# A three-block transformer kernel: the Fourier branch folded by symmetry, and half of a later layer's modulation computed in another stage

## The chip, the cores and the metric

The kernel runs on one core of one Trainium2 chip. The metric is the device time in microseconds of one execution; times without a unit are microseconds. PE is TensorE, PEld its weight load, DVE VectorE, ACT ScalarE, POOL GpSimd, SP SyncE, whose queue issues most DMAs. PS is the PSUM, eight banks of 128 x 512 fp32. Steps are counted from 0; "step n" is the body of the attention's loop for n.

## The reference, cut to what matters

512 tokens of 1024 features pass through a first block (attention beside a Fourier branch, then a mixture of 32 experts) and a second one of two layers (an S5 state space mixer with a gated unit and an MLP; a Mamba-2 mixer and an MLP). The change touches two computations. The Fourier branch of the first block:

```
def fourier_mix(f, w_fourier):
    fg = f.reshape(b, n, N_FOURIER_GROUPS, FOURIER_GROUP_DIM)          # 512 tokens, 4 groups of 128
    fr = jnp.fft.fft2(fg, axes=(1, 3), norm='ortho').real
    return jnp.einsum('bngc,gcd->bngd', fr, w_fourier)
```

and the modulation of the second block's first layer:

```
mod = silu(c) @ ada_w[i] + ada_b[i]                                    # 1024 -> 6 x 1024
sh1, sc1, g1, sh2, sc2, g2 = split(mod, 6)
h = rmsnorm(x) * (1 + sc1) + sh1;  x = x + g1 * s5_mixer(h)            # ends in val * sigmoid(gate)
h = rmsnorm(x) * (1 + sc2) + sh2;  x = x + g2 * mlp(h)
```

## The kernel before

Activations lie features-first: 128 features on the partitions, 512 tokens along the row. All engines run programs written out by hand; each engine works through its own list in order, and semaphores tie the lists together. There is no planner: what stands earlier in an engine's list is done earlier.

**The attention** has four heads of four query tiles, sixteen steps n (`hd = n // 4`, `qc = n % 4`). In each step TensorE computes the scores of step n (`scores`, L931), turns the weights of step n-1 in two parts (`turn_weights`, L943), and between these does other work: in steps 0 to 3 the values' projections (`values`), in steps 4 to 7 the four groups of Fourier features (`to_mix`, both end in L840), in steps 8 to 13 the Fourier branch, in steps 14 and 15 parts of the output projection (`out_part`, L969). The values of a head are summed in steps 1 and 2 of the next head (`head_values`, L957); for heads 1 and 2 this waits for `head_done`, the scaling of the head before on DVE. DVE takes the maximum (`maxima`, L2234), ACT the two exponentials (`exps`, L1664), DVE the weights (`attention_weights`, L2242 to L2248); scores of step n wait for the exponentials of step n-1. At steps 8 and 12 DVE and ACT also finish a head's norm: `head_var` (DVE), `head_root` (ACT, with a load of the root's table), `head_scale` (DVE, a 512-column reciprocal L2260 and the product L2263).

**The Fourier branch**, per group: `mix_channels` multiplies the features by a 128 x 256 table of cosines and sines (four matmuls of 256 columns), ACT copies the result (`mixed_channels`), `mix_tokens` multiplies by the 512 x 512 cosine and sine tables over tokens (eight matmuls of 512 columns, L908 and L909), ACT copies (`mixed_tokens`), `mix_out` applies `w_fourier` (L916), ACT copies (`mixed_out`).

**Modulation** is a dot product on DVE: blocks of 128 output features, each a 128 x 1024 tile of transposed weights times the broadcast condition, summed along the row (`mod_block`, L2230). All 48 blocks of the layer are done in the attention, three a step, from two buffers; GpSimd issues their DMAs (L613) as `ada_used` frees a buffer. SyncE issues the expert weights only behind the last head's values and the last block.

**The gated unit** follows the S5 mixer: two halves i of the features, each as 4 value tiles (s = 0, banks 0 to 3) and 4 gate tiles (s = 1, banks 4 to 7), every product as three fp32r matmuls (L740 to L744). ACT takes the sigmoid of a gate tile (L1895), DVE the product with the value tile and the addition to x (L2677, L2680), which raises `glu_used`. TensorE writes bank k of the second half only when `glu_used` has reached k + 1. The norm ahead of the MLP needs all eight. The modulation of the second layer is done in the MLP, from `ada_buf1`.

## Time and profile before

| | |
|---|---|
| median of 3 runs (lowest, highest) | 2213.03 (2212.02, 2213.48) |
| the profiled execution's own time | 2213.58 |
| its span | 2211.9 |
| busy: PE, DVE, ACT, POOL | 2134.6, 1215.4, 702.6, 148.8 |
| DMA in the mean | 197 GB/s |
| attention, scores of step 0 to the turn of step 15's weights | 118.05 to 295.74 |
| gated unit on TensorE | 1004.11 to 1091.28 |

The profiler's page gives busy time by engine, granted TensorE clock, DMA load, the chain of work that ended last, and the costliest groups of instructions. Queries of the trace give the same for a stretch, and the instructions in order of time. Busy time of an engine off the chain costs nothing by itself. A matmul's busy time contains its way through the array; from the start of one to the start of the next is what it costs.

### The profile page before, as it was taken

The page shows a single profiled execution, that of the slowest core. Times are in us where ns is not written, and L with a number is a line of the kernel's source. Part 1 is how long each engine was busy: PE and PEld are TensorE (multiplying, and loading weights), DVE is VectorE, ACT ScalarE, POOL GpSimd, SP SyncE. Part 2 cuts the span into 40 slices and gives each one's busy share as a digit, 9 for nine tenths or more (in the row PEclk, how much of TensorE's full clock was granted, in tenths as well). Part 3 has the DMA queues.
Part 4 walks back from the last instruction along what each step waited for, and adds up shares of the span by engine and source line. Part 5 has one row for each costly group of instructions (what it writes and reads, how often), then busy time and mean ns, then how long its engine had stood idle before and what let it go on. Part 6 is the DMA issues. An engine that isn't in the chain of part 4 may idle for free.

```text
span 2211.9 us, 24806 instructions
## 1 busy us (share of the span) xinstructions
PE 2134.6 (97%) x9914; PEld 1428.7 (65%) x9914; DVE 1215.4 (55%) x1726; ACT 702.6 (32%) x1059; POOL 148.8 (7%) x157
## 2 busy tenths in 40 slices
PE   7999998997999989999999999999999999999997
PEld 3454444333333335678888888878777788888886
DVE  1776863344433336895474555566986646343434
ACT  4123422110000005323242231346884424232331
POOL 0011100002310004000000000000110000000000
PEclk9999999999999999999999999999999999999999
DMA  9756465999999993211345454423342222222221
GB/s 389 288 185 215 142 241 208 401 427 427 420 426 426 428 427 127 79 68 62 133 160 186 156 177 163 143 77 116 126 156 81 96 95 77 95 95 95 95 96 57
DMA packets 112808, 434.71 MB, mean 197 GB/s; under 512 B 7982, under 2 KB 13106, under 8 KB 98760
## 3 DMA queue, kind: packets, MB, share of 16 engines
q1 hardware_dynamic: 92872, 361.46, 42.6%
q0 software_dynamic: 19840, 71.93, 9.0%
q8 instruction: 66, 1.08, 0.2%
q14 instruction: 30, 0.25, 0.0%
HBM read 430.57 MB, written 6.36 MB: 198 GB/s over the span
## 4 chain that ended last, share of the span: by engine, by line
PE 60%; PEld 15%; DVE 7%; DMA 7%; issue 6%; ACT 2%; DVEq 2%; POOLq 0%; SPq 0%; PEldq 0%; POOL 0%; ACTq 0%
PE PS L1132 7%; PE PS L740 6%; PE PS L743 6%; PE PS L744 6%; PE PS L840 6%; PEld PS L740 5%; PEld PS L744 5%; PEld PS L743 4%; DMA work<-in_w_dn 4%; PE PS L1155 4%; PE PS L1399 3%; PE PS L1403 3%; PE PS L1402 3%; PE PS L1169 2%; PE PS L969 2%
## 5 line engine op out<-in xcount | busy, mean ns | idle before, releaser
L744 PE MATMUL PS<-work_f32r,work_f32r 128*128 128x512 f32 x1168 | 454.4, 389 | 0.0
L2155 DVE TENSOR_TENSOR ring_f32r<-ring,work_f32r 128x2048 fp32r<-128x2048 f32 x100 | 227.8, 2287 | 140.5 <-ACT work_f32r L1553 140.1
L740 PE MATMUL PS<-work_f32r,work_f32r 128*128 128x512 f32 x768 | 299.5, 390 | 2.1 <-DVE work_f32r L2902 1.1
L743 PE MATMUL PS<-work_f32r,ring_f32r 128*128 128x512 f32 x768 | 298.8, 389 | 0.0
L1553 ACT ACTIVATE work_f32r<-ring 128x2048 fp32r<-128x2048 f32 x100 | 190.2, 1910 | 304.0 <-DMA ring<-in_mlp_w 247.0
L744 PEld LDWEIGHTS PS<-work_f32r,work_f32r 128*128 128x128 f32 x1168 | 219.3, 188 | 45.6
L1132 PE MATMUL PS<-work 128*64 128x512 f32 x752 | 170.6, 597 | 2.2 <-ACT work L1761 2.2
L740 PEld LDWEIGHTS PS<-work_f32r,work_f32r 128*128 128x128 f32 x768 | 144.2, 188 | 33.3 <-DVE work_f32r L2902 1.5
L743 PEld LDWEIGHTS PS<-work_f32r,ring_f32r 128*128 128x128 f32 x768 | 144.2, 188 | 29.8 <-issue 0.2
L740 PE MATMUL PS<-h_f32r,work_f32r 128*128 128x512 f32 x400 | 155.9, 390 | 1.4 <-DVE work_f32r L2175 1.4
L743 PE MATMUL PS<-h_f32r,ring_f32r 128*128 128x512 f32 x400 | 155.6, 389 | 0.0
L2472 DVE SCALAR_TENSOR_TENSOR x<-PS,mod,x 128x512 f32<-128x512 f32 x128 | 90.1, 746 | 68.7 <-PE PS L1169 68.3
L1771 ACT ACTIVATE work<-PS 128x256 f32<-128x256 f32 x32 | 12.3, 383 | 360.3 <-PE PS L1132 360.3
L2717 DVE SCALAR_TENSOR_TENSOR x<-PS,mod,x 128x512 f32<-128x512 f32 x64 | 48.1, 751 | 137.2 <-PE PS L744 137.0
L1399 PE MATMUL PS<-h_f32r,work_f32r 128*128 128x512 f32 x288 | 120.7, 419 | 0.0
L1132 PEld LDWEIGHTS PS<-work 128*64 128x64 f32 x752 | 51.3, 137 | 101.9 <-issue 100.9
L1553 ACT ACTIVATE work<-PS 128x512 f32<-128x512 f32 (+2 forms) x94 | 50.8, 550 | 198.8 <-PE PS L840 85.9
L1403 PE MATMUL PS<-work_f32r,work_f32r 128*128 128x512 f32 x288 | 112.6, 391 | 0.0
L1402 PE MATMUL PS<-h_f32r,ring_f32r 128*128 128x512 f32 x288 | 112.4, 390 | 0.0
L2708 DVE TENSOR_SCALAR work<-PS 128x512 f32<-128x512 f32 x64 | 43.9, 691 | 116.0 <-PE PS L744 116.0
L1155 PE MATMUL PS<-work 128*64 128x512 f32 x384 | 94.7, 610 | 6.1 <-DMA work<-in_w_dn 5.4
L1925 ACT ACTIVATE work_f32r<-work 128x512 fp32r<-128x512 f32 x64 | 40.4, 631 | 171.4 <-DVE work L2708 171.4
(423 smaller groups left out, 3357.8 us busy)
## 6 DMA issues: line engine op xcount, KB each, us to landing
work<-in_w_gu SPq DMA_DIRECT2D x47, 2048.0 KB, 21.9
ring<-in_mlp_w SPq DMA_DIRECT2D x64, 1024.0 KB, 5.2
work<-in_w_dn SPq DMA_DIRECT2D x24, 2048.0 KB, 24.6
ring<-in_w_gu SPq DMA_DIRECT2D x16, 2048.0 KB, 24.2
work<-in_ada_w_2T POOLq DMA_DIRECT2D x48, 512.0 KB, 3.6
work<-in_ada_w_2T POOLq DMA_DIRECT2D x16, 1536.0 KB, 6.8
ring<-in_m_w_in SPq DMA_DIRECT2D x20, 1024.0 KB, 5.2
work<-in_w_adaT POOLq DMA_DIRECT2D x8, 2048.0 KB, 10.4
```

The source lines that it names most:

```text
L740: mm = nc.tensor.matmul(PS[:, bank + k, :], f32r(w_of), f32r(hi(c)), start=first and c == 0, stop=False)
L743: nc.tensor.matmul(PS[:, bank + k, :], f32r(wlo), f32r(hi(c)), start=False, stop=False)
L744: mm = nc.tensor.matmul(PS[:, bank + k, :], f32r(w_of), f32r(lo(c)), start=False, stop=last and c == 3)
L840: mm = nc.tensor.matmul(PS[:, bank, 0:n], cols_of(c), rhs_of(c), start=(c == 0), stop=(c == KC - 1))
L1132: mm = nc.tensor.matmul(PS[CAP * half:CAP * (half + 1), 2 + s, :], xbT[:, 4 * part + c, CAP * s:CAP * (s + 1)], w[:, c, half * 512:(half + ...
L1155: mm = nc.tensor.matmul(PS[CAP * s:CAP * (s + 1), 5 + n, :], hidT[:, s, k % 2, CAP * (k // 2):CAP * (k // 2 + 1)], tiles[s][0][:, k, n * 5 ...
L1399: mm = nc.tensor.matmul(PS[:, k, :], f32r(w_of), f32r(h[:, c, :]), start=(c == 0), stop=False)
L1402: nc.tensor.matmul(PS[:, k, :], f32r(wlo), f32r(h[:, c, :]), start=False, stop=False)
L1403: mm = nc.tensor.matmul(PS[:, k, :], f32r(w_of), f32r(xbc_h_lo[:, c, :]), start=False, stop=(c == KC - 1))
L1553: return nc.scalar.activation(out, in_, ACT.Copy)
L2155: tt(f32r(ring[:, s, at, :]), ring[:, s, at, :], f32r(tiles[s][:, at, :]), ALU.subtract).then_inc(w_split, 1)
L2472: stt(x[:, c, :], PS[:, SCATTER_BANKS[c % 2], :], mod1[:, 5 * KC + c:5 * KC + c + 1], x[:, c, :], ALU.mult, ALU.add).then_inc(x2_added, 1)
```

## The change

The Fourier branch uses that the cosine over 512 tokens is even and the sine odd about token 256. DVE folds a group of features into an even and an odd part of 256 tokens (`fold_tokens`, steps 6 to 9; token 256 is kept apart, in `f_half`), reading the later half backward (`mirrored`). TensorE then needs five matmuls of 128 columns over channels and five of 257 or 255 columns over tokens. The result is the even part for frequencies 0 to 256 and the odd part for 1 to 255; DVE adds and subtracts them (`unfold_frequencies`, steps 9 to 12, ahead of `head_scale`), again writing backward. The four groups take steps 9 to 12, one each, with `mix_out` one step later; values are spread over steps 0 to 4, `to_mix` over 5 to 8, and the output projection begins in step 13.

Of the 48 modulation blocks the first 24 stay in the attention (the S5 mixer's shift, scale and gate), at most two a step as `BLOCKS_AT` says. The other 24, for the MLP, move into the gated unit as 12 pairs (`mod_pair`), two pairs ahead of each of the gates 0 to 5, from two buffers of 1 MB that GpSimd fills after the S5 mixer's last matmul. The bias and the norm's gain follow ahead of gate 6. One semaphore now counts two stores that had two.

```diff
-ADA_BLOCKS = NMOD * KC
-ADA_DONE = ADA_LATE + ADA_BLOCKS
+ADA_BLOCKS = 3 * KC
+ADA_GLU = (NMOD * KC - ADA_BLOCKS) // 2
+ADA_DONE = ADA_LATE + ADA_BLOCKS + ADA_GLU
...
-        dft_c, dft_s, dft_ch = wk(13312, TC, T), wk(15360, TC, T), wk(17408, 256)
-        fab, fre = wk(17664, 2, 4, 256), wk(19712, T)
+        dft_c, dft_s, dft_ch = wk(13312, 3, 257), wk(14088, 2, 255), wk(17408, 256)
+        f_odd, f_half, fab, fre = wk(14600, GROUPS, 256), wk(16648, GROUPS, P), wk(15624, 2, 4, P), wk(19712, T)
...
+        FIRST_MIX = 9
...
+        ada_pair = [wk(24576, 2, D), wk(26624, 2, D)]
...
+        def mirrored(v):
+            n = v.ap[-1][1]
+            return bass.AP(v.tensor, v.offset + n - 1, [v.ap[0], (-1, n)])
...
-            sp.wait_ge(ada_used, 2 + ADA_DONE)
+            sp.wait_ge(ada_used, 2 + ADA_LATE + ADA_BLOCKS)
...
+            pool.wait_ge(s5_mm, KC)
+            for j in range(ADA_GLU):
+                pool.wait_ge(ada_used, 2 + ADA_LATE + ADA_BLOCKS + max(j - 1, 0))
+                pool.dma_start(ada_pair[j % 2], A["ada_w_2T"][0, (ADA_BLOCKS + 2 * j) * P:(ADA_BLOCKS + 2 * j + 2) * P, :]
+                               .rearrange("(n p) k -> p n k", p=P)).then_inc(ada_loaded[j % 2], 16)
...
             def mix_channels(g):
+                pe.wait_ge(folded, g + 1)
                 if g:
-                    pe.wait_ge(fourier_evac, 4 * (g - 1) + FR)
+                    pe.wait_ge(fourier_evac, 3 * (g - 1) + FO)
                 else:
                     pe.wait_ge(in_mix, 16 * 6)
                     pe.wait_ge(qkv_evac, 22)
-                for t in range(TC):
-                    if g and t == 2:
-                        pe.wait_ge(fourier_evac, 4 * (g - 1) + FO)
-                    mm = nc.tensor.matmul(PS[:, t // 2, (t % 2) * 256:(t % 2 + 1) * 256], fT[:, g, t * P:(t + 1) * P],
-                                          dft_ch, start=True, stop=True)
-                    if t % 2:
-                        mm.then_inc(fourier_mm, 1)
-            def mix_tokens(g, tiles):
-                pe.wait_ge(fourier_evac, 4 * g + AB)
-                for t in tiles:
-                    nc.tensor.matmul(PS[:, 0, :], fab[:, g % 2, t, 0:P], dft_c[:, t, :], start=(t == 0), stop=False)
-                    mm = nc.tensor.matmul(PS[:, 0, :], fab[:, g % 2, t, P:2 * P], dft_s[:, t, :], start=False,
-                                          stop=(t == TC - 1))
-                if t == TC - 1:
-                    mm.then_inc(fourier_mm, 1)
+                even, odd, cosines, sines = fT[:, g, :], f_odd[:, g, :], dft_ch[:, 0:P], dft_ch[:, P:2 * P]
+                for t in range(2):
+                    nc.tensor.matmul(PS[:, 0, t * P:(t + 1) * P], even[:, t * P:(t + 1) * P], cosines, start=True, stop=True)
+                nc.tensor.matmul(PS[:, 0, 3 * P:4 * P], odd[:, P:2 * P], sines, start=True, stop=True)
+                nc.tensor.matmul(PS[:, 0, 2 * P:3 * P], odd[:, 0:P], sines, start=True, stop=False)
+                nc.tensor.matmul(PS[:, 0, 2 * P:3 * P], f_half[:, g, :], cosines, start=False, stop=True).then_inc(fourier_mm, 1)
+            def mix_tokens(g):
+                pe.wait_ge(fourier_evac, 3 * g + AB)
+                if g:
+                    pe.wait_ge(folded, GROUPS + g)
+                for t in range(3):
+                    nc.tensor.matmul(PS[:, 1, 0:257], fab[:, g % 2, t, :], dft_c[:, t, :], start=(t == 0), stop=(t == 2))
+                for t in range(2):
+                    mm = nc.tensor.matmul(PS[:, 1, 257:512], fab[:, g % 2, 2 + t, :], dft_s[:, t, :], start=(t == 0), stop=(t == 1))
+                mm.then_inc(fourier_mm, 1)
             def mix_out(g):
-                pe.wait_ge(fourier_evac, 4 * g + FR)
-                nc.tensor.matmul(PS[:, 1, :], wfour[:, g, :], fre, start=True, stop=True).then_inc(fourier_mm, 1)
+                pe.wait_ge(folded, GROUPS + g + 1)
+                nc.tensor.matmul(PS[:, 0, :], wfour[:, g, :], fre, start=True, stop=True).then_inc(fourier_mm, 1)
...
-                if n in (9, 11, 12, 14):
-                    mix_out({9: 0, 11: 1, 12: 2, 14: 3}[n])
+                if FIRST_MIX < n <= FIRST_MIX + GROUPS:
+                    mix_out(n - FIRST_MIX - 1)
                 if n:
...
-                elif n == 1:
-                    values(2)
-                    values(3)
-                elif n == 2:
-                    values(4)
-                elif n == 3:
-                    values(5)
-                    tile_done()
-                    tile_wait("in", 1, 1)
-                elif n < 8:
-                    to_mix(n - 4)
-                    if n == 7:
+                elif n < 5:
+                    values(n + 1)
+                    if n == 4:
                         tile_done()
-                elif n in (8, 9, 11, 12):
-                    mix_channels({8: 0, 9: 1, 11: 2, 12: 3}[n])
-                elif n in (10, 13):
-                    mix_tokens({10: 1, 13: 3}[n], range(2, 4))
+                        tile_wait("in", 1, 1)
+                elif n < FIRST_MIX:
+                    to_mix(n - 5)
+                    if n == 8:
+                        tile_done()
+                elif n < FIRST_MIX + GROUPS:
+                    mix_channels(n - FIRST_MIX)
+                elif n == 13:
+                    tile_wait("out", 0, 0)
+                    pe.wait_ge(fourier_evac, 3 * 2 + FO)
+                    out_part(0, 1, OUT_ORDER[0:3])
                 elif n == 14:
-                    tile_wait("out", 0, 0)
                     pe.wait_ge(head_done, 2)
+                    pe.wait_ge(fourier_evac, 3 * 3 + FO)
                     out_part(0, 0, OUT_ORDER[0:5])
                 elif n == 15:
-                    pe.wait_ge(fourier_evac, 4 * GROUPS)
-                    out_part(0, 1, OUT_ORDER[0:6])
+                    out_part(0, 1, OUT_ORDER[3:6])
...
-                if n in (8, 11):
-                    mix_tokens({8: 0, 11: 2}[n], range(4))
-                elif n in (9, 12):
-                    mix_tokens({9: 1, 12: 3}[n], range(2))
+                if FIRST_MIX <= n < FIRST_MIX + GROUPS:
+                    mix_tokens(n - FIRST_MIX)
...
             def mixed_channels(g):
-                for b in range(2):
-                    act.wait_ge(fourier_mm, 4 * g + b + 1)
-                    if g >= 2:
-                        act.wait_ge(fourier_mm, 4 * (g - 2) + FR)
-                    copy(fab[:, g % 2, 2 * b:2 * b + 2, :], PS[:, b, :].rearrange("p (t n) -> p t n", n=256)) \
-                        .then_inc(fourier_evac, 1)
+                act.wait_ge(fourier_mm, 3 * g + AB)
+                copy(fab[:, g % 2, :, :], PS[:, 0, :].rearrange("p (t n) -> p t n", n=P)).then_inc(fourier_evac, 1)
             def mixed_tokens(g):
-                act.wait_ge(fourier_mm, 4 * g + FR)
-                copy(fre, PS[:, 0, :]).then_inc(fourier_evac, 1)
+                act.wait_ge(fourier_mm, 3 * g + UV)
+                copy(fre[:, 0:257], PS[:, 1, 0:257]).then_inc(fourier_evac, 1)
             def mixed_out(g):
-                act.wait_ge(fourier_mm, 4 * g + FO)
-                copy(h[:, HEADS + g, :], PS[:, 1, :]).then_inc(fourier_evac, 1)
+                act.wait_ge(fourier_mm, 3 * g + FO)
+                copy(h[:, HEADS + g, :], PS[:, 0, :]).then_inc(fourier_evac, 1)
...
-                if n in (9, 11, 12, 14):
-                    mixed_out({9: 0, 11: 1, 12: 2, 14: 3}[n])
+                if FIRST_MIX < n <= FIRST_MIX + GROUPS:
+                    mixed_out(n - FIRST_MIX - 1)
                 if n:
                     weights_turned(n - 1, 0)
-                if n in (8, 9, 11, 12):
-                    mixed_channels({8: 0, 9: 1, 11: 2, 12: 3}[n])
+                if FIRST_MIX <= n < FIRST_MIX + GROUPS:
+                    mixed_channels(n - FIRST_MIX)
                 exps(n)
                 if n == 0:
                     act.wait_ge(rope_done, 8)
                     projected(12)
                     projected(13)
-                elif n == 1:
-                    projected(14)
-                    projected(15)
-                elif n == 2:
-                    projected(16)
-                elif n == 3:
-                    projected(17)
-                elif n < 8:
-                    projected(14 + n)
-                elif n in (10, 13):
-                    mixed_tokens({10: 1, 13: 3}[n])
+                elif n < FIRST_MIX:
+                    projected(13 + n)
                 if hd and qc == 3:
                     head_square(hd - 1)
                 if n:
                     weights_turned(n - 1, 1)
                 if hd >= 2 and qc == 0:
                     head_root(hd - 2)
-                if n in (8, 11):
-                    mixed_tokens({8: 0, 11: 2}[n])
+                if FIRST_MIX <= n < FIRST_MIX + GROUPS:
+                    mixed_tokens(n - FIRST_MIX)
...
+            def fold_tokens(g):
+                dve.wait_ge(qkv_evac, 18 + g + 1)
+                early, late = fT[:, g, 1:T // 2], mirrored(fT[:, g, T // 2 + 1:T])
+                tt(f_odd[:, g, 1:T // 2], early, late, ALU.subtract)
+                nc.vector.tensor_copy(f_half[:, g, 0:1], fT[:, g, T // 2:T // 2 + 1])
+                tt(early, early, late, ALU.add).then_inc(folded, 1)
+            def unfold_frequencies(g):
+                dve.wait_ge(fourier_evac, 3 * g + UV)
+                early, late, odd = fre[:, 1:T // 2], mirrored(fre[:, T // 2 + 1:T]), PS[:, 1, 257:512]
+                tt(late, early, odd, ALU.subtract)
+                tt(early, early, odd, ALU.add).then_inc(folded, 1)
+            BLOCKS_AT = (1, 2, 2, 2, 2, 2, 2, 1, 0, 2, 2, 1, 0, 2, 2, 1)
             for n in range(HEADS * TC):
                 hd, qc = n // TC, n % TC
                 maxima(n)
                 if n == 0:
                     modulation((5, ADA_TILES // 2), -MOD_EARLY // 4, cond1, col("b_ada", 0, 48), mod1)
-                    attention_weights(0)
-                    for q in range(3):
-                        mod_block(q)
-                    continue
+                    nc.vector.memset(f_odd[:, :, 0:1], 0.0)
+                    nc.vector.memset(f_half, 0.0)
+                if FIRST_MIX - 3 <= n < FIRST_MIX + 1:
+                    fold_tokens(n - FIRST_MIX + 3)
                 if hd >= 2 and qc == 0:
                     head_var(hd - 2)
                 if hd and qc == 3:
                     head_out(hd - 1)
-                mod_block(3 * n)
-                mod_block(3 * n + 1)
+                first, count = sum(BLOCKS_AT[:n]), BLOCKS_AT[n]
+                ahead = min(2, count) if n else 0
+                for q in range(first, first + ahead):
+                    mod_block(q)
                 attention_weights(n)
-                mod_block(3 * n + 2)
+                for q in range(first + ahead, first + count):
+                    mod_block(q)
+                if FIRST_MIX <= n < FIRST_MIX + GROUPS:
+                    unfold_frequencies(n - FIRST_MIX)
                 if hd >= 2 and qc == 0:
...
+            def mod_pair(j):
+                dve.wait_ge(ada_loaded[j % 2], 16 * ((ADA_LATE + ADA_BLOCKS) // 2 + j // 2 + 1))
+                for n in range(2):
+                    w, q = ada_pair[j % 2][:, n, :], ADA_BLOCKS + 2 * j + n
+                    done = stt(w, w, 1.0, cond2[:], ALU.mult, ALU.mult, accum_out=mod2[:, 0, q:q + 1])
+                done.then_inc(ada_used, 1)
             split_weight_half("glu", 0, 0, 0, glu_tiles)
             outputs_rest(KC - 2)
             outputs_rest(KC - 1)
             for i in range(2):
                 split_weights("glu", 4 + 2 * i, i, glu_tiles)
                 for n in range(4 * i, 4 * i + 4):
+                    if n < ADA_GLU // 2:
+                        mod_pair(2 * n)
+                        mod_pair(2 * n + 1)
+                    elif n == ADA_GLU // 2:
+                        dve.drain()
+                        late = slice(ADA_BLOCKS, NMOD * KC)
+                        tt(mod2[:, 0, late], mod2[:, 0, late], col("ada_b0", ADA_BLOCKS, NMOD * KC - ADA_BLOCKS), ALU.add)
+                        dve.drain()
+                        norm_gain(4, mod2[:, 0, 4 * KC:5 * KC], "nmlp0")
                     dve.wait_ge(gate_sig, n + 1)
...
+    def half_rows(a):
+        a = a.astype(f)
+        rest = np.zeros((P, a.shape[1]), f)
+        rest[0] = a[T // 2]
+        return np.ascontiguousarray(np.concatenate([a[0:T // 2], rest]).reshape(3, P, -1).transpose(1, 0, 2))
     return {
         "mats": mats, "rope_c": np.cos(ang).astype(f), "rope_s": np.sin(ang).astype(f),
-        "dft_c": token_rows(np.cos(tt) * ortho), "dft_s": token_rows(-np.sin(tt) * ortho),
+        "dft_c": half_rows(np.cos(tt)[:, 0:257] * ortho), "dft_s": half_rows(-np.sin(tt)[:, 1:256] * ortho)[:, 0:2],
```

## Rows read from the trace of the kernel before

**Rows 1.** The page, part 1: engine, busy time, instructions

```profile
PE 2134.6 (97%) x9914; PEld 1428.7 (65%) x9914; DVE 1215.4 (55%) x1726; ACT 702.6 (32%) x1059; POOL 148.8 (7%) x157
```

**Rows 2.** The chain that ended last, attention: start, length, piece of the chain

```profile
133.54 1.49 PE PS L931 x8
...
135.03 0.48 PE PS L943 x3
...
149.25 0.33 PE PS L943 x3
...
151.54 6.87 PE PS L840 x16
...
163.71 3.53 DMA work<-in_ada_w_2T
...
167.27 1.24 DVE work L2230 x2
...
200.13 2.58 PE PS L957 x6
...
215.84 1.74 PE PS L900 x8
...
220.24 0.86 PE PS L908 x2
...
295.74 0.52 PE PS L943 x3
```

**Rows 3.** Timeline of TensorE: start, length, instructions merged, idle time before and releaser

```profile
546.54 1.97 PE L1115 MATMUL PS<-mats_sb,work 128*128 128x128 f32 x8 [8.47 <-DMA work<-h_rows,idx_all]
...
1004.11 0.47 PE L740 MATMUL PS<-work_f32r,work_f32r 128*128 128x512 f32 x1 [0.32 <-DVE ring_f32r L2155]
...
1091.28 2.84 PE L729 MATMUL PS<-ones 128*128 128x128 f32 x24
```

**Rows 4.** Timeline of DVE, gated unit

```profile
1033.32 2.29 DVE L2155 TENSOR_TENSOR ring_f32r<-ring,work_f32r 128x2048 fp32r<-128x2048 f32 x1 [8.72 <-ACT work_f32r L1553]
...
1040.52 0.75 DVE L2677 SCALAR_TENSOR_TENSOR work<-PS,cols_sb,work 128x512 f32<-128x512 f32 x1 [4.90 <-ACT work L1895]
...
1041.34 1.15 DVE L2680 SCALAR_TENSOR_TENSOR x<-work,mod,x 128x512 f32<-128x512 f32 x1
...
1084.04 0.75 DVE L2677 SCALAR_TENSOR_TENSOR work<-PS,cols_sb,work 128x512 f32<-128x512 f32 x1 [26.57 <-ACT work L1895]
```

**Rows 5.** Timeline of DVE, step 8 of the attention; last two from the S5 mixer

```profile
215.41 1.76 DVE L2234 TENSOR_REDUCE sm<-PS 128x2 f32<-128x1536 f32 x1 [2.39 <-PE PS L931]
...
222.59 0.16 DVE L2242 RECIPROCAL sm<-sm 128x2 f32<-128x2 f32 x1
...
223.60 1.02 DVE L2248 SCALAR_TENSOR_TENSOR work<-work,sm 128x768 f32<-128x768 f32 x1
...
224.53 1.22 DVE L2230 SCALAR_TENSOR_TENSOR work<-work,cond 128x1024 f32<-128x1024 f32 x1
...
225.68 3.35 DVE L2260 RECIPROCAL norm_buf<-norm_buf 128x512 f32<-128x512 f32 x1
...
960.22 0.43 DVE L2589 TENSOR_TENSOR work<-work 128x256 f32<-128x256 f32 x1
...
960.56 0.42 DVE L2590 TENSOR_TENSOR work<-work 128x256 f32<-128x256 f32 x1
```

**Rows 6.** Timeline of ACT, step 8 of the attention

```profile
218.10 0.89 ACT L1664 ACTIVATE work<-PS,sm 128x768 f32<-128x768 f32 x1
...
220.37 1.28 ACT L1682 ACT_TABLE_LOAD   x1
...
221.66 0.63 ACT L1682 ACTIVATE norm_buf<-norm_buf 128x512 f32<-128x512 f32 x1
```

**Rows 7.** DMA issues: count, size, median from issue to landing

```profile
work<-in_ada_w_2T POOLq DMA_DIRECT2D x16, 1536.0 KB, 6.8
```

**Rows 8.** Windows: PE, PEld, DVE, ACT, POOL busy, granted clock, DMA share, GB/s

```profile
544.00:546.00 2.00, 0.00 (x0) 0.00 (x0) 0.00 (x0) 0.00 (x0) 0.00 (x0) 0.50 1.01 424
```

More of the change, by code:

```diff
@@ L330, in build @@
         qkv_mm, qkv_evac, rope_mm, rope_done = sem("qkv_mm"), sem("qkv_evac"), sem("rope_mm"), sem("rope_done")
-        fourier_mm, fourier_evac = sem("fourier_mm"), sem("fourier_evac")
-        AB, FR, FO = 2, 3, 4
+        fourier_mm, fourier_evac, folded = sem("fourier_mm"), sem("fourier_evac"), sem("folded")
+        AB, UV, FO = 1, 2, 3
         score_mm, negmax_ready, exp_done, a_ready = sem("score_mm"), sem("negmax_ready"), sem("exp_done"), sem("a_ready")
@@ L337, in build @@
         head_done, x1_ready, out_stored = sem("head_done"), sem("x1_ready"), sem("out_stored")
-        zero_row_stored, route_mm = sem("zero_row_stored"), sem("route_mm")
+        route_mm = sem("route_mm")
         tok_mm, routing_evac, rows_stored = sem("tok_mm"), sem("routing_evac"), sem("rows_stored")
@@ L457, in _ @@
             sp.dma_start(h_rows[T:T + 1, :].rearrange("o (q n) -> o q n", n=256),
-                         zeros[0:1, :].unsqueeze(1).broadcast_to([1, 4, 256])).then_inc(zero_row_stored, 16)
+                         zeros[0:1, :].unsqueeze(1).broadcast_to([1, 4, 256])).then_inc(rows_stored, 16)
             sp.wait_ge(pv_mm, HEADS)
-            sp.wait_ge(ada_used, 2 + ADA_DONE)
+            sp.wait_ge(ada_used, 2 + ADA_LATE + ADA_BLOCKS)
             sp.dma_start(w_router, A["w_router"]).then_inc(in_late, 16)
@@ L480, in _ @@
                     sp.dma_start(h_rows[0:T, :].rearrange("(t p) d -> p t d", p=P), tok_rows).then_inc(rows_stored, 16)
-                    sp.wait_ge(rows_stored, 16)
+                    sp.wait_ge(rows_stored, 32)
                     sp.wait_ge(route_mm, 5)
@@ L613, in _ @@
                 pool.dma_start(ada_block[q % 2], A["ada_w_2T"][0, q * P:(q + 1) * P, :]).then_inc(ada_loaded[q % 2], 16)
-            pool.wait_ge(zero_row_stored, 16)
-            pool.wait_ge(rows_stored, 16)
+            pool.wait_ge(rows_stored, 32)
             pool.wait_ge(idx_set, 1)
@@ L2288, in _ @@
             head_var(HEADS - 1)
-            tt(mod2[:, 0, :], mod2[:, 0, :], col("ada_b0", 0, 48), ALU.add)
+            tt(mod2[:, 0, 0:ADA_BLOCKS], mod2[:, 0, 0:ADA_BLOCKS], col("ada_b0", 0, ADA_BLOCKS), ALU.add)
             dve.drain()
@@ L2292, in _ @@
             norm_gain(3, mod2[:, 0, KC:2 * KC], "nmix0")
-            norm_gain(4, mod2[:, 0, 4 * KC:5 * KC], "nmlp0")
             dve.drain()
```

2 lines of the change are left out of this document (removed).

## The prediction

> **What bounds the kernel now.** I read the page first: TensorE is busy for 97% of the span [rows 1], so a change counts by what it does to TensorE's own queue, and by what TensorE is made to wait for. The chain of waits in the attention comes second. It runs through TensorE piece after piece, sixteen steps of one query tile each. Step 1 starts at 133.54, and the turn of step 15's weights starts at 295.74 [rows 2]. All that TensorE issues there counts: scores 1.49, two turns of weights 0.48 and 0.33, a projection 6.87, half a head's values 2.58 [rows 2]. Its waits in this stretch, in the timeline, come to only about 5 us. After it TensorE never rests until the router, and the expert stream is issued from SyncE behind the last head, so a shift of 295.74 moves all later work by as much. Third, the timelines of DVE and TensorE in the gated unit: TensorE issues 384 matmuls from 1004.11 to 1091.28 without a wait, 0.227 each, so 2.72 for the twelve of one output tile and half [rows 3]. DVE has little to do there up to 1040, but then its gates (0.75 and 1.15) follow each other at just that pace from 1084.04 [rows 4].
>
> **Part 1, less TensorE work in the attention.** A 512-column fp32 matmul is two instructions, 0.86 [rows 2]. Per group before: channels 1.74 (four of 256 columns), tokens eight of 512 columns, 6.88, output 0.86; together 9.5. After: five of 128 columns. The warming matmuls have that shape, 2.84 for 24 instructions, 0.118 each [rows 3], so 1.18. Tokens 3x257 + 2x255 = 1281 columns, 2.15. Output 0.86. Together 4.2, so 5.3 less, 21 for four groups. With the old waits of 5 gone, step 15's turn could come 26 earlier. New waits give part of that back; so I walk the steps on the clock of this trace.
> - Steps 1 to 4 now hold one projection each: 1.49+0.48+6.87+0.33 = 9.17, step 5 starts at 170.2. DVE needs less per step (maximum 1.76+0.17, two modulation blocks 2.3, weights 2.0 [rows 5]), and two blocks in flight ahead cover the 3.9 from release to use [rows 2]: no wait. Steps 5 and 6 add 2.58, step 7 a norm sum of 0.86 and its wait of 0.6, step 8 is 9.17: step 9 starts at 213.6.
> - Step 9: head 1's values wait for head 0's scaling (head_done). ACT must take in the last projection (213.3+0.6) and a turn, then load the root's table 1.28 and take the root, 0.63 [rows 6]: 216.3. The reciprocal 3.35 [rows 5] and the scaling, 0.75 as any such operation [rows 4], end at 220.4. TensorE is there at 217.1: **wait 3.4**. Tokens end at 225.3, step 10 starts.
> - DVE of step 9 starts only at 220.4: maximum 1.9, fold 0.8, two blocks 2.3, weights 2.0, unfold 0.8 = 228.2. A fold is two operations of 255 columns and a tiny one; one of 256 columns takes 0.42 and the next starts 0.34 behind it [rows 5], so 0.8 for a fold or an unfold. mix_out(0) behind the scores of step 10 (226.8) **waits 1.5**. Steps 10 to 12 are then 10.7, 8.0 and 6.8 long with small waits of 0.5 in all: step 13 at 250.8.
> - Step 12 has an unfold and the scaling of head 1 in one: unfold ends at 254.2 (ACT did the table and root, 1.9, ahead of its copy), scaling at 258.3. mix_out(3) **waits 1.9**; the maximum of step 13 starts at 258.3, exponentials 0.89 x 2 [rows 6] end at 262.1, step 14 **waits 1.0** and its turn behind DVE (two blocks, weights) **0.9**. Step 15 starts at 272.2; norm sum, one block and weights end at 279.5, against a TensorE ready at 278.9.
> So step 15's turn comes at 279.6 rather than 295.74: **-16.1**. Bounds: -21 if the waits go as they were, -12 if the unknown forms cost more. The backward read of a tile is in no row; below, nothing more than the 0.34; above, the 0.69 or so that a 512-column operation takes, which is 0.7 more on each of four unfolds, three of them on the path: +2. I take 0.34, the same operation on as many columns.
>
> **Part 2, 24 blocks of modulation into the gated unit.** The DVE work there was under TensorE's waits or beside them; it now costs by its place. Twelve pairs: a block is 1.22 and the next starts 1.15 behind it [rows 5], so 2.3 a pair; twelve GpSimd DMAs of 1 MB. 0.5 MB took 3.53 [rows 2] and 1.5 MB 6.8 [rows 7] from issue to landing, so 5.2 between them, and 0.4 from release to issue: 5.6 from the end of pair j-2 to the start of pair j. Before gate n (n = 0 to 5) DVE does two pairs.
> - Gate 0: pairs 0 and 1 were loaded long ago (issued at about 1003). DVE runs them from 1035.6, behind the split of 1033.32, to 1040.2; the gate at 1040.52 is not late [rows 4]. Cost 0.
> - Pair 2 starts at 1037.9+5.6 = 1043.5, pair 3 at 1045.8; gate 1 ends at 1050.1. Pairs 4 and 5 from 1051.4 and 1053.7, gate 2 ends at 1058.0. Pairs 6 and 7 from 1059.3 and 1061.6, gate 3 ends at 1065.9. The second half of the unit writes the banks that these gates read: its tiles 1, 2, 3 are due at 1050.3, 1053.0 and 1055.8. Tile 1 is met; tile 2 waits 5.0; tile 3, by then due at 1060.8, waits 5.2. **+10.2**. Queued behind the waiting matmul is all of TensorE's second half. Below: pairs always loaded in time, 4.6+2.0 per gate, gate 3 ends at 1062.3, +6.6. Above: 6.8 as for 1.5 MB, because the MLP's first tiles load beside them: +13 to +14.
> - Pairs 8 and 9 lie ahead of gate 4 in 26 us of idle DVE: 0. Pairs 10 and 11 lie between gates 4 and 5, where the gates already follow back to back from 1084.04: 4.6. Adding the bias and the gain ahead of gate 6: 0.5. The norm that follows hangs on the last gate: **+5.1**.
> The Trainium skill (DMA: Bandwidth & Descriptors, "Anatomy of one DMA — SWDGE (gpsimd) path") gives 2.0 us plus bytes over 436 GB/s for such a DMA: an estimate of 4.4 for 1 MB, 3.2 and 5.6 for the two sizes in the rows, which took 3.5 and 6.8. By the page's 4.4 the first term would be 7.8 rather than 10.2. The trace is above the page at both sizes, so I stay with the rows.
>
> **Part 3, TensorE's clock.** In the experts TensorE stood still for 8.5 up to 546.5; the granted clock was 0.50, which is 1.2 GHz, from 544 to 546 [rows 8], and the eight turns of 128 columns that followed took 1.97, which at 0.118 would be 0.95 [rows 3]. The gated unit had no such stop before. Its first new stop falls into the second; the second costs up to 1.9, I take 1.1. At its end, TensorE now waits some 7 for the last square instead of 1.7: the sums, the warming matmuls and the spread run at half speed, about 1.9 by the same row. **+3.0** (0 to 5). The 3.4 of step 9 is shorter and mostly beside DVE: +0.4.
>
> **Rest.** The two cosine and sine tables shrink by 1.3 MB at a time when TensorE runs without a wait on DMA: 0. One semaphore counts two stores instead of two: 0. Norm gain 4 leaves the attention's end, beside ACT's root: 0. The two clearings of step 0, at most 0.7, lie ahead of weights due at 135.0 and done at 133.3: 0.
>
> **Sum.** -16.1+10.2+5.1+3.0+0.4 = +2.6 against the profiled execution, 2213.58 (span 2211.9 and 1.7 around it). That execution is 0.5 above the median of 2213.03. So 2215.6 for a median.
>
> **The rivals.** A difference under 0.2% (4.4 us) can't be told from none.
> - *Slower: the gated unit's DVE queue costs more than the folding earns.* Place: the wait of tiles 2 and 3 for gates 2 and 3. Loads of 6.8 (+3.5), both stops at half clock (+2), a colder end (+1.5): 2215.6+7 = 2222.6. It decides from a load of about 6.3 us. For: MLP tiles load in the same stretch, and the 1.5 MB loads have such company. Against: 0.5 MB loads beside other tiles still took 3.6 mostly. Chance 0.28.
> - *Faster: waits of the new order overlap less badly.* TensorE's attention queue gives -20 (head 0's scaling meets step 9 in time), the pairs land early (+6.6), the clock holds (+1): -20+6.6+5.1+1 = -7.3, 2205.7. For: the arithmetic of columns is certain, 21. Against: ACT's order puts the root behind the projection of step 8. Chance 0.16.
> - *The fold does not pay: backward reads or the short fp32 matmuls cost far above their shape.* At four times the price, unfold 3.2, each mix_out waits 2 more and each step's maximum too, +8 to +10: 2225. Nothing in the profile speaks for it, nothing excludes it. Chance 0.08.
> - *Forecast: the two parts cancel*, 2211 to 2218: 0.48.
>
> **Numbers.** Predicted 2215.6. Range 2206.5 to 2223: the bounds -21/+6.6/0 clock below, -12/+13/+5 above, cut where under 2 in 10 is left. Forecast's own range 2210 to 2219. Faster 0.16, same 0.48, slower 0.36.
>
> **What would show it.** In the attention: turn of step 15's weights at 280 (278 to 284); steps 1 to 4 at 9.2; a wait of about 3 at step 9's head values on DVE, and waits of mix_out on DVE in steps 10 and 13. Experts and S5 the same length, just earlier. In the gated unit: two TensorE waits of about 5 on DVE's gates (L2680's successor), DVE waiting for DMA ahead of pairs 2, 4 and 6, granted clock below 1.00 behind them; last gate 15 later against the unit's start. Wrong would be: no TensorE wait in the unit's second half, or a turn of step 15 before 276 or behind 286.

## The result: slower by 0.5%

The changed kernel takes 2224.21 us (median of 5, 2222.28 to 2227.34) against 2213.03 (median of 5, 2212.02 to 2215.51): ratio 1.005, 95% interval 1.0035 to 1.0065. Forecast was 2215.6, range 2206.5 to 2223. Its profiled execution took 2222.28 with a span of 2220.2: 8.3 longer than the 2211.9 of before. It was the fastest of the five. The medians differ by 11.2 and the two profiled executions by 8.7, so 2.5 us of the difference are not in these traces.

TensorE has less to do, and its share of the span falls [rows 1]:

```profile
PE 2120.6 (96%) x9898; PEld 1427.5 (64%) x9898; DVE 1220.8 (55%) x1749; ACT 699.9 (32%) x1055; POOL 144.6 (7%) x145
```

TensorE's timeline at the ends of the attention and in step 9 (start, length, instructions merged; in brackets the idle time before, and what ended it):

```profile
132.07 1.56 PE L944 MATMUL PS<-work 64*128 64x512 f32 x8
...
220.22 4.51 PE L970 MATMUL PS<-work 128*128 128x512 f32 x6 [3.38 <-DVE h L2258]
...
281.61 0.52 PE L956 MATMUL PS<-mats_sb,work 128*128 128x128 f32 x3 [0.51 <-DVE work L2243]
```

Step 1 begins at 132.07 (133.47 in the timeline of before, 133.54 in its chain) and the turn of step 15 at 281.61 (295.74) [rows 2]. The earlier begin is no effect of the change: in a second profile of the changed kernel (changed_again below) it was 133.28, and over all kernels below it lay between 132.1 and 133.7. In step 9 there is the wait that the prediction walked to, 3.4 us for head 0's scaling. Here are the fold of group 1 and the unfold of step 9 on DVE; each fold reads its later half backward, and the first unfold operation writes backward:

```profile
196.19 0.42 DVE L2263 TENSOR_TENSOR work<-work 128x255 f32<-128x255 f32 x1
...
227.35 0.42 DVE L2270 TENSOR_TENSOR work<-work,PS 128x255 f32<-128x255 f32 x1 [0.42 <-ACT work L1561]
227.69 0.41 DVE L2271 TENSOR_TENSOR work<-work,PS 128x255 f32<-128x255 f32 x1
```

The gated unit. First TensorE's waits from 985 to 1115 (who waited <- for whom: total us, times, longest), first of the kernel before, where there was none for a gate, and then of the changed one; then TensorE's timeline; then DVE's (before: [rows 4]):

```profile
PE PS L791 <- DVE work L2119: 1.7, 1, 1.7
```

```profile
PE PS L752 <- DVE x L2710: 13.0, 3, 9.0
PE PS L803 <- DVE work L2114: 6.6, 1, 6.6
```

```profile
1038.47 0.50 PE L752 MATMUL PS<-work_f32r,work_f32r 128*128 128x512 f32 x1 [1.55 <-DVE x L2710]
...
1050.45 0.79 PE L752 MATMUL PS<-work_f32r,work_f32r 128*128 128x512 f32 x1 [8.97 <-DVE x L2710]
...
1058.42 0.50 PE L752 MATMUL PS<-work_f32r,work_f32r 128*128 128x512 f32 x1 [2.48 <-DVE x L2710]
```

```profile
1031.67 1.22 DVE L2686 SCALAR_TENSOR_TENSOR work<-work,cond 128x1024 f32<-128x1024 f32 x1 [2.88 <-DMA work<-in_ada_w_2T]
...
1037.28 1.13 DVE L2710 SCALAR_TENSOR_TENSOR x<-work,mod,x 128x512 f32<-128x512 f32 x1
1042.21 1.23 DVE L2686 SCALAR_TENSOR_TENSOR work<-work,cond 128x1024 f32<-128x1024 f32 x1 [3.80 <-DMA work<-in_ada_w_2T]
...
1046.13 1.23 DVE L2686 SCALAR_TENSOR_TENSOR work<-work,cond 128x1024 f32<-128x1024 f32 x1 [1.54 <-DMA work<-in_ada_w_2T]
...
1049.26 1.14 DVE L2710 SCALAR_TENSOR_TENSOR x<-work,mod,x 128x512 f32<-128x512 f32 x1
...
1086.67 0.75 DVE L2707 SCALAR_TENSOR_TENSOR work<-PS,cols_sb,work 128x512 f32<-128x512 f32 x1 [18.53 <-ACT work L1890]
```

DVE multiplies pairs (L2686) between its gates (L2710) and itself waits for their loads; TensorE waits for the gates; and ahead of gate 4 DVE idles 18.5 us. The last gate's product starts 109.4 behind the unit's first matmul, where it was 88.1: 21.3 later, not the 15 of the prediction.

The stages show where the time went. A stage is read from one start to the next in each kernel's timelines: the attention from the scores of step 1 to the last turn of step 15's weights, everything up to the gated unit's first matmul, from there to gate 4, and on to the first operation of the norm behind it.

| kernel | attention | between | unit to gate 4 | gate 4 to norm |
|---|---|---|---|---|
| before | 165.2 | 705.4 | 79.9 | 16.3 |
| changed | 152.5 | 705.8 | 96.3 | 22.0 |
| changed_again | 151.8 | 705.8 | 98.0 | 22.1 |
| fold_only | 162.9 | 705.4 | 79.9 | 16.3 |
| move_only | 162.3 | 705.1 | 96.9 | 22.6 |
| pairs_in_idle | 152.5 | 707.3 | 80.2 | 16.5 |
| two_pair_loads | 152.5 | 704.3 | 87.7 | 22.3 |
| half_loads | 152.5 | 708.2 | 89.9 | 22.5 |
| warm | 152.5 | 704.7 | 94.8 | 22.0 |
| tail_early | 151.8 | 709.7 | 97.8 | 16.3 |
| root_first | 147.3 | 711.0 | 98.8 | 22.6 |
| scale_first | 158.2 | 703.6 | 97.4 | 22.3 |
| fold_two_loads | 156.8 | 708.4 | 79.9 | 16.3 |
| both | 147.3 | 704.6 | 80.2 | 16.0 |

Changed less before, taken before rounding: -1.4 up to step 1, -12.7, +0.4, +16.4, +5.7: the 8.3 of the spans. "Between" is the same work in all of them, yet it lay between 703.6 and 711.0. The clock has a part in that: in windows of 10 us from 640 to 1000 it fell short of full speed at places that differ by execution, by 10.2 us in sum in root_first (711.0) and 5.1 in the changed kernel (705.8); in scale_first, the shortest, it was 6.9, so that is not all of it. Hence single terms are read from the stages, and medians only confirm them.

### The profile page after: what moved, and what is told of

It reads as the page before. It is cut to its first block, busy times and chain, and to the rows that moved or that the text cites. A ratio compares the mean times of both kernels' runs of the same rounds, so it can differ in the third digit from the quotient of the medians.

```text
span 2220.2 us, 24786 instructions
## 1 busy us (share of the span) xinstructions
PE 2120.6 (96%) x9898; PEld 1427.5 (64%) x9898; DVE 1220.8 (55%) x1749; ACT 699.9 (32%) x1055; POOL 144.6 (7%) x145
## 4 chain that ended last, share of the span: by engine, by line
PE 59%; PEld 15%; DVE 8%; DMA 7%; issue 6%; ACT 2%; DVEq 2%; SPq 0%; POOLq 0%; PEldq 0%; POOL 0%; ACTq 0%
PE PS L1140 7%; PE PS L852 6%; PE PS L752 6%; PE PS L756 5%; PE PS L755 5%; PEld PS L752 5%; PEld PS L756 5%; PEld PS L755 4%; DMA work<-in_w_dn 4%; PE PS L1163 4%; PE PS L1407 3%; PE PS L1411 3%; PE PS L1410 3%; PE PS L982 2%; PE PS L1177 2%
## 5 line engine op out<-in xcount | busy, mean ns | idle before, releaser
L1561 ACT ACTIVATE work<-PS 128x512 f32<-128x512 f32 (+3 forms) x90 | 47.6, 539 | 186.0 <-PE PS L852 86.5
```

The lines of the kernel that those rows point to most:

```text
L1561: return nc.scalar.activation(out, in_, ACT.Copy)
```

## The experiments

Each was timed beside the kernel before, whose median was 2213.55, 2213.60, 2213.73 and 2213.31 in the four groups of runs. Ratios are to the kernel before; diffs are against the changed kernel unless said.

**fold_only**: the 48 blocks back in the attention.

```
-ADA_BLOCKS = 3 * KC
+ADA_BLOCKS = NMOD * KC
-BLOCKS_AT = (1, 2, 2, 2, 2, 2, 2, 1, 0, 2, 2, 1, 0, 2, 2, 1)
+BLOCKS_AT = (3,) * 16
```

> The changed kernel with the 48 blocks of the MLP's modulation all in the attention again, three to a step, and nothing of them in the gated unit. Theory A (TensorE set the attention's time, so the fold is worth what it takes from TensorE): the 12.7 to 14.1 us that the attention lost stay lost, less a little where VectorE, which now has fold, unfold and blocks, is late: 2199 to 2204 against 2213. Theory B (a good part of the attention's gain came from the 24 blocks that left it, 24 x 1.15 us of VectorE and 12.6 MB of loads): under half of the gain stays, 2206 to 2211, and waits of TensorE for VectorE stand in every step.

2211.5, ratio 0.9986 (0.9977 to 0.9995): theory B, at 0.5 above its range. Of the attention's 12.7 us only 2.3 come without moving blocks. What DVE and TensorE waited for from 130 to 300:

```profile
DVE work L2225 <- DMA work<-in_ada_w_2T: 16.6, 17, 3.7
DVE sm L2229 <- PE PS L944: 7.0, 6, 2.8
```

```profile
PE PS L929 <- DVE work L2271: 3.9, 3, 1.7
...
PE PS L944 <- ACT work L1668: 3.3, 2, 2.4
PE PS L956 <- DVE work L2243: 2.7, 3, 1.5
```

TensorE's waits for DVE's weights and unfolds stand in six places, not in every step as theory B had it. DVE, with shorter steps for as many blocks, hardly waits for scores (7.0 us; 17.0 in the kernel before, 29.7 in the changed one): it has become the bound, held up itself by the blocks' loads. The next run but one tests this.

**move_only** (against the kernel before): its own Fourier branch, and 24 blocks in the gated unit.

```
+ADA_BLOCKS = 3 * KC
...
-                mod_block(3 * n)
-                mod_block(3 * n + 1)
+                for q in range(first, first + count):
+                    mod_block(q)
```

> The kernel before with its own Fourier branch, and only the 24 blocks moved into the gated unit, placed there as in the changed kernel. Theory A: the attention stays within 2 us of before, the gated unit and what follows cost what they cost in the changed kernel (8.3 + 13.7 = 22 us), so 2231 to 2235. Theory B: the attention shortens by 5 us or more, so 2224 to 2229.

2233.42, ratio 1.0089 (1.0075 to 1.0103). The attention gains 2.9, more than the 2 of theory A and less than the 5 of theory B; the unit and its tail lose 23.2. So -2.3 and -2.9 alone, and -12.7 together: the fold frees TensorE, and only with half of the blocks off DVE's queue can the steps follow.

**fold_two_loads** (against fold_only): which of the two it is, the blocks' loads or their multiplications. Only two of the 48 loads, products times 0.

```
-            for q in range(ADA_BLOCKS):
+            for q in range(2):
```

> The kernel with the fold and all 48 blocks in the attention (fold_only) with only the first two of the 48 loads; the multiplications go on over the same data with a factor of 0, so the first layer's modulation is its bias alone. VectorE's order and work are those of fold_only. Theory D (with the fold the blocks' loads bound the attention, since VectorE idled 16.6 us for them there): the attention comes to that of the changed kernel, 2199 to 2203. Theory E (VectorE's own 24 x 1.15 us more bound it): 2208 to 2211, and the waits of TensorE for the softmax in steps 1 and 2 stand.

2207.85, ratio 0.9974 (0.9965 to 0.9984), between the theories: the attention is 156.8. Loads are 6.1 of the 10.4 us (162.9 to 152.5) between fold_only and the changed kernel, DVE's own work 4.3.

**two_pair_loads**: the gated unit without ten of its twelve loads.

```
-            for j in range(ADA_GLU):
+            for j in range(2):
```

> The changed kernel with only the first two of the 12 pair loads; the other ten pairs of multiplications are done on the same data, so the last 20 columns of the first layer's modulation are not the reference's. VectorE's order is unchanged, and no pair after the second waits for a load. By the prediction's terms the loads were 5.2 of 10.2 us, with some of the clock: 2217 to 2219. By the trace of the changed kernel VectorE idled 9.6 us for four pairs ahead of gates 1 to 3 (2.9, 3.8, 1.5, 1.4), all of it in front of TensorE's wait for gate 3, and the half clock goes with them: 2210 to 2213. If the loads were covered anyway: within 2 us of 2224.

2214.46, ratio 1.0002 (0.9993 to 1.0011), in none of the three ranges. Gate 4 comes at 87.7, 8.6 earlier, but the loads are worth more than that. The product of gate 3 starts 55.85 behind the unit's first matmul in place of 66.00, 10.15 earlier. From gate 3 to gate 4 it took 31.9 in place of 30.3, 1.6 more, and the granted clock behind the last wait was low here, where it was 1.00 in the changed kernel's profile (busy PE, PEld, DVE, ACT, POOL; granted clock; DMA share, GB/s):

```profile
1050.00:1055.00 5.00, 5.00 (x20) 4.06 (x19) 5.00 (x5) 0.00 (x0) 0.00 (x0) 0.81 0.21 38
```

So of the 16.4 us, 10.2 are waits for loads and 6.2 stay by DVE's order; the 7.8 that this run still shows hold 1.6 of clock.

**half_loads**: half of the bytes, all else the same.

```
+                count = 2 if j < 2 else 1
+                pool.dma_start(ada_pair[j % 2][:, 0:count, :],
```

> The changed kernel in which the loads of pairs 2 to 11 bring only the first of their two blocks (0.5 MB for 1 MB); the second multiplication of these pairs goes over what lies there, so ten columns of the first layer's modulation are not the reference's. Number and order of all instructions are unchanged. Theory F (a pair's load takes its 7 to 10 us because several MB share the DMA engines): VectorE idles under 3 us for the pairs ahead of gates 1 to 3 in place of 9.6, and gate 4 comes 6 us or more earlier against the unit's start: 2214 to 2218. Rival G (the time from a release to the use is mostly fixed, whatever is loaded): it idles 6 us or more, 2220 to 2224.

2217.93, ratio 1.002 (1.001 to 1.0029); gate 4 at 89.9, 6.4 earlier. DVE idled 3.6 us for loads instead of 9.6: nearer to F. The run halves each load and its neighbours together, so it does not tell a load's own bytes from its company. The DMA issues from 1020 to 1060 (count, size, median to landing), the changed kernel and then half_loads:

```profile
work<-in_ada_w_2T POOLq DMA_DIRECT2D x8, 1024.0 KB, 6.2
ring<-in_w_glu SPq DMA_DIRECT2D x2, 1024.0 KB, 6.0
```

```profile
work<-in_ada_w_2T POOLq DMA_DIRECT2D x8, 512.0 KB, 4.0
```

**pairs_in_idle**: the same pairs in the idle stretches.

```
             split_weights("glu", 2, 1, glu_tiles)
+            mod_pair(0)
+            mod_pair(1)
             for i in range(2):
-                split_weights("glu", 4 + 2 * i, i, glu_tiles)
+                split_weight_half("glu", 4 + 2 * i, i, 0, glu_tiles)
+                if i == 0:
+                    mod_pair(2)
+                    mod_pair(3)
+                split_weight_half("glu", 4 + 2 * i, i, 1, glu_tiles)
+                for j in range((4, 6)[i], (6, 12)[i]):
+                    mod_pair(j)
```

> The changed kernel with the same 12 pairs of blocks in stretches of the gated unit in which VectorE idled (10.9, 8.5 and 18.5 us): pairs 0 and 1 after the split of the second tile, 2 and 3 between the halves of the third, 4 and 5 after it, the other six with bias and gain after the split of the fourth, ahead of gate 4; nothing between gates 0 to 3 or 4 to 7. Theory A (only the place of the pairs cost the time, not their work nor their bytes): no wait of TensorE for a gate, no half clock, no tail: 2224 - 22 = 2200 to 2204. Rival C (the 12.6 MB beside the unit's own weights is the cost): the weight tiles land later, TensorE waits for their splits, 2207 to 2216. The prediction's own terms (10.2 + 5.1 + 3.0) would give 2206.

2201.42, ratio 0.9942 (0.9929 to 0.9956): theory A. TensorE's waits from 985 to 1095, where 13.0 and 6.6 stood:

```profile
PE PS L803 <- DVE work L2114: 1.8, 1, 1.8
```

The unit and its tail take 0.4 more than before. Its loads landed no sooner (median 6.9) and DVE waited 14.1 us for them, where nobody waited for DVE.

**tail_early**: pairs 10 and 11 with bias and gain ahead of gate 4.

```
-                    if n < ADA_GLU // 2:
+                    if n < 4:
...
+                    elif n == 4:
+                        for j in range(8, ADA_GLU):
+                            mod_pair(j)
```

> The changed kernel with only the tail's part moved: pairs 10 and 11 go with pairs 8 and 9 ahead of gate 4, and bias and gain behind them, where VectorE idled 18.5 us; gates 4 to 7 follow each other with nothing between. If the tail is 5.1 us of pairs, bias and gain and what TensorE loses behind its stop (together 5.7 to 6.0 by the traces of the changed kernel and of two_pair_loads): 2218 to 2219.5. If another wait takes the place of the pairs (the load of pairs 10 and 11 reaching gate 4): 2221 or more.

2221.32, ratio 1.003 (1.002 to 1.0041), above the 2218 to 2219.5 that I had put down. The last stage is 16.3 again, as before, so the tail cost 5.7, and no other wait took its place: gate 4 came at 97.8, as in changed_again (98.0). By the median only 2.9 came off; "between" was 709.7 in the profiled execution.

**warm**: idle matmuls ahead of three waits.

```
                     if freed is not None:
+                        if warm is not None:
+                            keep_warm(4, warm[k])
                         pe.wait_ge(*freed(k))
```

> The changed kernel with 48 idle multiplications of 128x128 on TensorE (5, 34 and 9, on a bank that is free there) ahead of its waits for the gates 1, 2 and 3, nothing else. They fill some 10 of the 13 us of wait. Theory A (the half clock behind the waits is a cost of its own, about 3 us): 2220.5 to 2222. Rival: the clock behind the waits costs nothing, since TensorE is waiting for the next gate again: 2223.5 to 2225.

2221.22, ratio 1.004 (1.0026 to 1.0054): by its number theory A, but the trace gives the half clock less. Windows of the second half (busy PE, PEld, DVE, ACT, POOL; granted clock; DMA share, GB/s), of the changed kernel, then its repetition, then warm:

```profile
1045.00:1050.00 5.00, 0.00 (x0) 0.00 (x0) 3.78 (x6) 0.00 (x0) 1.32 (x2) 0.63 0.63 213
1050.00:1055.00 5.00, 4.55 (x11) 3.58 (x12) 3.58 (x6) 0.00 (x0) 0.71 (x1) 0.50 0.72 216
...
1060.00:1065.00 5.00, 5.00 (x24) 4.14 (x23) 5.00 (x5) 0.00 (x0) 0.00 (x0) 1.00 0.72 250
```

```profile
1060.00:1065.00 5.00, 5.00 (x18) 3.99 (x17) 5.00 (x3) 0.00 (x0) 0.00 (x0) 0.74 0.45 174
```

```profile
1050.00:1055.00 5.00, 4.39 (x29) 3.81 (x27) 4.32 (x7) 0.00 (x0) 0.72 (x1) 1.00 0.60 208
```

From gate 3 to gate 4 it was 30.25 in warm and 30.28 in the changed kernel: the half clock from 1050 to 1055 cost nothing there, since TensorE then waited for gate 3 anyway. In the repetition the clock was low behind the last wait too, and that stretch took 31.9, as in four other kernels with such waits; root_first's took 32.9. So the clock cost 0, 1.6 or 2.6 by execution. The rest of warm's stage (1.4 less up to gate 3) goes with 1.5 us less of load waits (8.1 for 9.6).

**root_first**: one move on ScalarE.

```
                 exps(n)
+                if hd >= 2 and qc == 0:
+                    head_root(hd - 2)
...
-                if hd >= 2 and qc == 0:
-                    head_root(hd - 2)
```

> The changed kernel with one move on ScalarE: the square root of head 0 (with its table load, 1.28 + 0.63 us) right behind the exponentials of step 8, ahead of the copy of the last projection, and that of head 1 likewise in step 12. Theory A (the wait of 3.4 us for head_scale(0) in step 9 comes from the root that stands behind a copy of 7 us of projection, and the cold clock behind the wait costs a further 1.9): step 9 goes from 13.5 to 8.5 to 9.5 us, the time from 2224.2 to 2218.5 to 2220.5. Rival: the four instructions of VectorE behind head_scale (maxima, fold, two blocks) or the softmax of step 9 then bind, and under 2 us are gained: 2222 to 2224.

2222.91, ratio 1.0038 (1.0024 to 1.0052), in the range of the rival. Step 9 takes 8.2 in place of 13.5, and the attention 147.3: theory A for the stage (-5.2). The median shows only 1.3 of it beside the changed kernel's first; "between" took 711.0 in the profiled execution, and the unit 2.6 more, all of it from gate 3 to gate 4. The same move on top of pairs_in_idle (both, below) takes 5.2 off the median. Step 9 without the wait:

```profile
216.97 2.74 PE L970 MATMUL PS<-work 128*128 128x512 f32 x6
```

**scale_first**: unfold behind the scaling in step 12.

```
-                if FIRST_MIX <= n < FIRST_MIX + GROUPS:
-                    unfold_frequencies(n - FIRST_MIX)
                 if hd >= 2 and qc == 0:
                     head_scale(hd - 2)
+                if FIRST_MIX <= n < FIRST_MIX + GROUPS:
+                    unfold_frequencies(n - FIRST_MIX)
```

> The changed kernel with the unfolding of step 12 behind the scaling of head 1 instead of ahead of it (in no other step are there both). The walk through the steps in the prediction puts 4.1 us of VectorE (reciprocal and scaling) ahead of the unfold then, mix_out(3) in step 13 waits for it 1.2 + 4.1 = 5.3, step 14's values and step 14's waits for the exponentials get no better: 2224.2 + 3 to + 4.5, 2227 to 2229. Rival: the softmax of step 13 is what binds there, so the order inside step 12 makes no difference: 2223.5 to 2225.

2231.22, ratio 1.0077 (1.0064 to 1.0091); the attention 158.2, 5.8 more, outside what I had put down (3 to 4.5). Of that 1.0 lies in step 9, which the edit leaves alone: it took 14.5, at a granted clock of 0.50 from 222 to 226 behind the same wait of 3.38. Steps 13 and 14 take 4.8 more. The wait of mix_out(3) is there, and the clock behind it was 0.50, so its two matmul instructions took 2.08 in place of 1.12:

```profile
262.19 2.08 PE L929 MATMUL PS<-work 128*128 128x512 f32 x2 [5.03 <-DVE work L2271]
```

**both**: pairs_in_idle and root_first together.

> The pairs in VectorE's idle stretches and the root behind the exponentials, in one kernel. If the two act in different places, they add: 2201.4 - 4.5 = 2195.5 to 2198.5. If the root is worth under 2 us, 2199.5 to 2201.5.

2196.2 (2193.89 to 2197.81), ratio 0.9921 (0.9907 to 0.9934): faster than the kernel before by 17 us and than the changed one by 28. In its stages the two effects stand side by side, 147.3 and 80.2 with 16.0.

**changed_again**: the changed kernel once more.

> The changed kernel itself, beside the kernel before on the same chip, to see how far its steps repeat: 2221 to 2227, the attention from the scores of step 1 to the last turn 152.5 us, gate 4 at 94 to 97 us and the norm at 116 to 119 us behind the start of the gated unit. The stage between, in which the changed kernel does the same work as before, is expected to vary by some us from one execution to the next, as it did in the kernels so far (703.6 to 711.0 us).

2224.61, ratio 1.0055 (1.0042 to 1.0069). Gate 4 and the norm came later than I had put down (98.0, 120.1), by the 1.6 of clock behind the last wait. In its step 9:

```profile
221.43 2.81 PE L970 MATMUL PS<-work 128*128 128x512 f32 x6 [3.38 <-DVE h L2258]
```

The same wait, 3.38, as in the first profile, but the six matmuls took 2.81 in place of 4.51. Step 9 is 1.7 shorter by it (11.8), but step 10 is 1.0 longer (10.8 for 9.8), because mix_out(0) now waits for the unfold, as it did not in the first profile:

```profile
228.86 1.13 PE L929 MATMUL PS<-work 128*128 128x512 f32 x2 [0.96 <-DVE work L2271]
```

So the low clock of step 9 cost the attention 0.7 (152.5 against 151.8), not 1.7.

## Why the prediction was wrong

The mechanisms were right, and their sizes were not. The forecast was +2.6 on the profiled execution; the four stages give +9.7. The step that failed most is the time from a pair's release to its next use, put at 5.6 and measured at up to 9.7: +5 of the 7 us. The attention's waits are the other 3, and the tail came out 1.3 cheaper.

- **Waits for the gates, +10.2 and 1.1 of clock; measured +16.4.** The failed term is the 5.6 from the end of a pair to the start of pair j+2. It was 7.5 for pair 2, then 8.3 and 9.7 for pairs 4 and 5, and 5.7 for pair 7. Pairs 2 and 3 were freed 2.5 us apart, and their successors loaded beside each other and beside weight tiles of the unit; no run separates the two. I had interpolated between two sizes, 3.53 and 6.8 [rows 2, 7], and left the load's company out. With loads on time I had said 6.6, and two_pair_loads gives 6.2 up to its last gate wait; what loads add, 3.6 by my sum, is 10.2. The 1.1 of clock was not there in the first profile, and 1.6 in the second. The slower rival had this mechanism, and named a load of 6.3 as the point from which it decides; the median landing was 6.2, but DVE waited for those of pairs 2, 4 and 5, of 7.1, 7.9 and 9.3 from issue to use.
- **The Trainium skill** (DMA: Bandwidth & Descriptors, "Anatomy of one DMA — SWDGE (gpsimd) path") gives 4.4 for 1 MB and 3.2 for 0.5 MB, as estimates from its figures: the trace was above it again, 6.2 and 4.0 here. It describes one DMA by itself, and the term of 7.8 that it gave was off by more than the 10.2 of the rows.
- **Attention, -16.1 and +0.4 of clock; measured -12.7.** The wait of 3.4 at step 9, its cause on ScalarE and the lengths of steps 1 to 3 came out as walked (root_first removes the wait). In the second profile, where the clock held in step 9, the attention is still 2.7 longer than walked. Of that 1.2 lie in steps 1 to 8 (step 4 took 9.6, not 9.2; step 7 11.2, not 10.6; step 8 9.5), and 1.8 in steps 11 and 12 (8.8 and 7.8, not 8.0 and 6.8). There "small waits of 0.5 in all" failed: TensorE waited 2.1 for ScalarE's copies in steps 10 to 12 (three times 0.45, twice 0.36). Steps 13 and 14 were 0.7 shorter than walked: mix_out(3) waited 1.2 and not 1.9. Steps 9, 10 and 15 were within 0.3. "Mostly beside DVE" failed in its place more than in its size: the clock was 0.57 from 220 to 224, behind the wait, when TensorE was at work, and cost step 9 1.7; step 10 gave 1.0 of it back, because its wait for the unfold (put at 1.5, 1.0 in the second profile) fell away. That leaves 0.7 for my 0.4.
- **"DVE needs less per step": right, and worth more than its sentence.** I priced the fold at 21 us of TensorE's work and the blocks' leaving at nothing in the attention. fold_only and move_only show that the fold alone is worth 2.3 there: the other 10.4 us hung on the blocks that left. The walk had both parts in it, so this changes what earned the time, and no term of the sum.
- **Tail, +5.1, and 1.9 of clock; measured +5.7 in all.** The 5.1 was right: 5.0 up to the last gate, and tail_early takes the whole 5.7 back. The granted clock was 0.59 and 0.72 from 1100 to 1110, but from the last gate to the norm only 0.7 was lost.
- **Rivals.** "The fold does not pay" is refuted: a backward read of 255 columns took 0.42, a forward one of 256 0.42 to 0.43 [rows 5]. "Faster" needed the head's scaling in time and the pairs landed early; each had to be made (root_first, pairs_in_idle).
- **The median** lies 1.9 above the profiled execution, which had no clock loss behind its last gate wait; six of the later profiles had one, of 1.6 to 2.6. That this is the 1.9 is not shown: the changed kernel's other four executions have no trace.
- **A reading.** The two tables shrink by 1.4 MB, not 1.3; nothing hangs on it.

## What to carry to other kernels

When work is moved off a busy engine's queue, price both halves by an experiment each: here a TensorE saving of 21 us brought 2.3 until DVE's queue was shortened too. Work moved into another stage costs by where it stands in the queue: the same twelve pairs cost 22 us ahead of operations that TensorE waits for, and 0.4 in the stretches where the queue was idle. Price a prefetch by its size and by what else loads at that moment, its own neighbours too: 1 MB with company took 7.1 to 9.3 us from issue to use where 5.2 had been put down. And when a run is to price one wait, read the stretch up to that wait: here the clock behind it hid 1.6 of 10.2 us.

## What the runs showed of the hardware

- The clock behind one and the same wait: TensorE stood still 3.38 us in step 9 in two executions of the same kernel. In one the granted clock then was 0.57 (2.4 GHz in part, 1.2 in part), in the other 1.00; the step took 13.5 and 11.8, and the attention 152.5 and 151.8, since a wait of 1.0 in the next step fell away.
- A low clock cost time only where no wait followed: a window at 0.50 cost nothing ahead of a further wait (30.25 and 30.28 from gate 3 to gate 4 with and without it), and one at 0.74 behind the last wait went with 1.6 us (31.90).
- VectorE reads a tile backward at the price of a forward read, and writes it so too: 0.42 for the fold's 255 columns, 0.42 and 0.41 for the two operations of the unfold, against 0.43 and 0.42 for 256 columns forward [rows 5].
